# A recurrence's doubling step: half of one head's products move to the other partition half, in six groups a level

## What is computed

```
def step(state, inp):
    r_t, w_t, k_t, v_t, kk_t, a_t = inp
    sa = jnp.einsum('bhvk,bhk->bhv', state, -kk_t)
    state = (state * w_t[:, :, None, :]
             + sa[..., None] * (kk_t * a_t)[:, :, None, :]
             + v_t[..., None] * k_t[:, :, None, :])
    y = jnp.einsum('bhvk,bhk->bhv', state, r_t)
    return state, y
```

## Time and profile before

| | |
|---|---|
| median of three runs | 2886.83 us (2880.5 to 2887.5) |
| span of the profiled execution | 2890.0 us; no other time of it is given |
| TensorE, VectorE, ScalarE, GpSimd busy | 2784.7, 1962.0, 1370.0, 1435.9 us |
| granted clock of TensorE, mean | 0.985 of full speed |
| the recurrence in the span | about 1680 to 2120 us |

### The profile page before, as it was taken

The page is one execution under the profiler, slowest core; times in us unless marked ns, Lnnn a source line. Parts: engine busy times, 40 slices in busy tenths (PEclk is TensorE's granted clock), DMA queues, the critical chain, the costliest instruction groups (busy, mean ns, idle before and its releaser), DMA issues.

```text
span 2890.0 us, 63578 instructions
## 1 busy us (share of the span) xinstructions
PE 2784.7 (96%) x25936; PEld 2218.1 (77%) x25936; DVE 1962.0 (68%) x2814; ACT 1370.0 (47%) x2296; POOL 1435.9 (50%) x961
## 2 busy tenths in 40 slices
PE   8898899999999999998999999999999999999998
PEld 6544567887888888876678878988878788888887
DVE  6587888689777777788132347776647766656667
ACT  5476877235334433346433345666414443334445
POOL 0001000233777767774446636675552576677772
PEclk9899999999999999999999999999999999999999
DMA  8200000532332322331442411222312112111111
GB/s 300 77 1 16 1 2 2 212 106 62 88 102 73 93 81 83 93 113 32 160 146 88 161 60 55 76 85 64 112 36 59 44 48 69 44 44 58 57 45 73
DMA packets 194397, 225.29 MB, mean 78 GB/s; under 512 B 14862, under 2 KB 151649, under 8 KB 194209
## 3 DMA queue, kind: packets, MB, share of 16 engines
q1 hardware_dynamic: 182529, 180.66, 20.2%
q10 hardware_dynamic: 11680, 42.01, 4.0%
HBM read 185.15 MB, written 37.22 MB: 77 GB/s over the span
## 4 chain that ended last, share of the span: by engine, by line
PE 72%; DVE 9%; ACT 4%; issue 3%; POOL 2%; DMA 0%; ACTq 0%; DVEq 0%; SPq 0%; POOLq 0%
PE ps L148 18%; PE ps L149 18%; PE ps L150 18%; PE ps L3849 3%; DVE uc L1090 2%; PE ps L3858 2%; PE ps L2304 2%; PE ps L2293 1%; PE ps L2315 1%; PE ps L3778 1%; PE ps L3856 1%; ACT d_r L2446 1%; PE ps L3838 1%; DVE d_r L2706 1%; POOL w_lo L738 1%
## 5 line engine op out<-in xcount | busy, mean ns | idle before, releaser
L148 PE MATMUL ps<-x_hi,w_hi 128*128 128x512 f32 x1160 | 453.3, 391 | 2.9 <-POOL w_lo L738 2.8
L150 PE MATMUL ps<-x_hi,w_lo 128*128 128x512 f32 x1160 | 451.5, 389 | 0.0
L149 PE MATMUL ps<-x_lo,w_hi 128*128 128x512 f32 x1160 | 451.4, 389 | 0.0
L738 POOL TENSOR_TENSOR w_lo<-w_room,w_hi 128x512 fp32r<-128x512 f32 x188 | 287.7, 1543 | 232.4 <-ACT w_hi L1252 232.4
L738 POOL TENSOR_TENSOR w_lo<-sq_room,w_hi 128x512 fp32r<-128x512 f32 x182 | 285.8, 1581 | 218.9 <-ACT w_hi L1252 218.9
L1090 DVE SCALAR_TENSOR_TENSOR uc<-u,pc,uc 128x1024 f32<-128x1024 f32 x176 | 327.4, 1871 | 25.9 <-ACT uc L1266 15.6
L1078 DVE TENSOR_TENSOR u<-u,ps 128x512 f32<-128x512 f32 x228 | 151.1, 683 | 195.3 <-PE ps L150 170.9
L148 PEld LDWEIGHTS ps<-x_hi,w_hi 128*128 128x128 f32 x1160 | 217.7, 188 | 50.5 <-POOL w_lo L738 5.7
L148 PE MATMUL ps<-g_hi,w_hi 128*128 128x512 f32 x640 | 250.3, 391 | 6.5 <-DVE h L1156 6.2
L150 PEld LDWEIGHTS ps<-x_hi,w_lo 128*128 128x128 f32 x1160 | 217.7, 188 | 45.6
L149 PEld LDWEIGHTS ps<-x_lo,w_hi 128*128 128x128 f32 x1160 | 217.8, 188 | 44.8
(11 more groups left out here) (493 smaller groups left out, 6876.2 us busy)
## 6 DMA issues: line engine op xcount, KB each, us to landing
w_room<-in_f_w_up_dram SPq DMA_DIRECT2D x48, 512.0 KB, 5.0
rwkv_scratch<-rp_stage ACTq DMA_DIRECT2D x48, 512.0 KB, 3.5
sq_room<-in_f_w_up_dram SPq DMA_DIRECT2D x40, 512.0 KB, 4.6
ada_w<-in_ada_w_dram SPq DMA_DIRECT2D x80, 256.0 KB, 2.8
rc_raw<-rwkv_scratch SPq DMA_DIRECT2D x28, 512.0 KB, 3.9
d_ada_w<-in_ada_w_dram SPq DMA_DIRECT2D x24, 512.0 KB, 7.7
d_r<-in_ada_w_dram ACTq DMA_DIRECT2D x24, 512.0 KB, 6.4
sq_room<-in_f_w_down_dram SPq DMA_DIRECT2D x24, 512.0 KB, 4.4
```

Of the source, the lines that this page charges most:

```text
L148: pe.matmul(out, w_hi, x_hi, start=first, stop=False, skip_group_check=skip)
L149: pe.matmul(out, w_hi, x_lo, start=False, stop=False, skip_group_check=skip)
L150: return pe.matmul(out, w_lo, x_hi, start=False, stop=last, skip_group_check=skip)
L738: pool.tensor_tensor(slot_of(k.w_lo, s), src, slot_of(k.w_hi, s).bitcast(F32), ALU.subtract).then_inc(w_lo_done, 1)
```

## The change

- Half of the second head's products (blocks 4 to 7) use the other partition half: `far(h, x, c)` gives the side, and `removed_pe` writes the first l there.
- A level on TensorE is six groups of 16 products. The loop is rotated: the z of level 1 stand ahead of it (`first_z`), the body makes u and l of a level and z of the next, four times, and the u of level 5 stand behind it (`last_u`). The l products of level 5 are dropped.
- The first head's u, z and the second head's l are copied in two parts of 256 columns (PARTS = 2, 1), and their banks move; all of PSUM is one tensor so that one copy can read two banks. The key sums are four products of 256 columns in halves of banks 2, 3, 5 and 6, and the second pair of them also waits for the copy of y.
- ScalarE's order: log and root of the pair before move from level 3, behind both heads' copies, to level 5, between the u copies of the first and second head. turn moves from level 2 to level 5.
- VectorE's order: the key maxima move ahead of the levels, s1 behind level 1, s2 behind level 4, scans into levels 2 and 3.

```diff
+    def far(h, x, c):
+        return c if h and x >= QUARTER else 1 - c
...
+    def z_of(pe, h, x, c):
+        i = x // QUARTER
+        out = bank(4 + i if h else 4 + 2 * i)[:, part(x, 1 - h if i == 0 else 0)]
+        return pe.matmul(out[hs(far(h, x, c)), :], tg[hs(c), x, h, G_M, :], ul[hs(c), 0, h, x, :],
+                         start=True, stop=True)
+
+    def u_of(pe, h, x, c):
+        side, i = hs(far(h, x, c)), x // QUARTER
+        out = bank(2 * h + i)[:, part(x)]
+        return pe.matmul(out[hs(c), :], ul[side, 1, h, x, :], z[side, h, x, :],
+                         start=False, stop=False, skip_group_check=True)
+
+    def l_of(pe, h, x, c):
+        side = hs(far(h, x, c))
+        out = bank(x // QUARTER)[:, part(x, 1)] if h else bank(7)[:, at(x)]
+        return pe.matmul(out[side, :], z[side, h, x, :], ul[side, 1, h, x, :],
+                         start=False, stop=False, skip_group_check=True)
...
+    def first_z(pe, p):
+        for i in range(2):
+            if i and p + 1 < PAIRS:
+                pe.wait_ge(sem["max"], 2 * p + 4)
+            for x in quarter(i):
+                for c in range(2):
+                    a_last = z_of(pe, 0, x, 1 - c)
+                    if i:
+                        z_of(pe, 1, x, c)
+            a_last.then_inc(sem["z_ps"][0], 1)
+        pe.wait_ge(sem["z_sb"][0], 10 * p + 1)
+        for x in quarter(0):
             for c in range(2):
...
+                last = z_of(pe, 1, x, c)
+        last.then_inc(sem["z_ps"][1], 1)
...
     def level_pe(pe, p, lv):
...
+        pe.wait_ge(sem["l_sb"][0], lv + 4 * p)
+        for i in range(2):
+            pe.wait_ge(sem["z_sb"][0], lv * 2 + (10 * p + i - 1))
+            pe.wait_ge(sem["l_sb"][1], lv * 2 + (8 * p + i - 1))
             begun(pe)
...
+            ul_a(pe, i)
+        pe.wait_ge(sem["z_sb"][1], lv + 5 * p)
+        begun(pe)
+        u_b(pe)
+        for i in range(2):
+            pe.wait_ge(sem["u_sb"][0], lv * 2 + (10 * p + i - 1))
             begun(pe)
...
+            z_a_l_b(pe, i)
+        pe.wait_ge(sem["u_sb"][1], lv + 5 * p)
+        pe.wait_ge(sem["z_sb"][0], lv * 2 + (10 * p + 1))
+        begun(pe)
+        z_b(pe)
+
+    def last_u(pe, p):
+        pe.wait_ge(sem["l_sb"][0], 4 * p + 5)
+        for i in range(2):
+            pe.wait_ge(sem["z_sb"][0], 10 * p + 9 + i)
+            pe.wait_ge(sem["l_sb"][1], 8 * p + 9 + i)
+            ul_a(pe, i, False)
+        pe.wait_ge(sem["z_sb"][1], 5 * p + 5)
+        u_b(pe)
...
             banks_opened(pe, p)
-            with pe.Fori(1, 6) as lv:
+            first_z(pe, p)
+            with pe.Fori(1, LV[-1]) as lv:
                 level_pe(pe, p, lv)
+            last_u(pe, p)
...
             for lv in LV:
...
+                u_act(act, p, lv, 0)
+                if p and lv == LV[-1]:
+                    log_act(act, p - 1)
+                    root_act(act, p - 1)
+                u_act(act, p, lv, 1)
+                if lv < LV[-1]:
+                    la_act(act, p, lv)
+                    lb_act(act, p, lv)
+                if more and lv in (1, 2):
+                    ln_act(act, q, lv - 1)
+                if more and lv in (3, 4):
+                    rs_act(act, q, lv - 3)
+                if lv == LV[-1]:
+                    turn_act(act, p, 0)
+                    turn_act(act, p, 1)
             tail_act(act, p)
...
+            if more:
                 for i in range(2):
...
+                    max_dve(dve, q, i)
             for lv in LV:
...
+                for h in range(2):
+                    levels_dve(dve, p, lv, h)
+                if p and lv == 1:
+                    for i in range(2):
+                        s1_dve(dve, p - 1, i)
+                if p + 2 < PAIRS and lv in (2, 3):
+                    scan_dve(dve, p + 2, lv - 2)
+                if p and lv == 4:
+                    for i in range(2):
+                        s2_dve(dve, p - 1, i)
```

More of the change, by code:

```diff
@@ L101, in alloc @@
     k.nm_small = [k.sb(f"nm_small{i}", [P, 3, TT]) for i in range(3)]
[L103 removed]
+    k.ps_all = stack.enter_context(nc.psum_tensor("ps", [P, 4, S], F32))
+    k.ps = [k.ps_all[:, i, :] for i in range(4)]
     k.w_room = k.sb("w_room", [P, 2, S])
@@ L3586, in rkw_act, with sums_of @@
         act.activation(rkw, heads2[:, :], ACT.Copy, scale=col("b_r_k", q)).then_inc(sem["bon"], 1)
+    def sums_of(q, i):
+        if q == 0:
+            return bank(6 + i).rearrange("p (b c) -> p b c", b=2)
+        return bank_pair((2, 5)[i], slice(HALF // 2, HALF))
     def max_dve(dve, q, i):
         dve.wait_ge(sem["sum"], 2 * q + i + 1)
-        dve.tensor_scalar(kk[:, halves(i)], bank(6 + i), 1e-24, None, ALU.max).then_inc(sem["max"], 1)
+        dve.tensor_scalar(kk[:, halves(i)].rearrange("p (b c) -> p b c", b=2), sums_of(q, i), 1e-24, None, ALU.max
+                          ).then_inc(sem["max"], 1)
     def kk_dve(dve, q, i):
@@ L3608, in sums_pe @@
         for i in range(2):
-            pe.matmul(bank(6 + i), same[:, :], kk[:, halves(i)], start=True, stop=True).then_inc(sem["sum"], 1)
+            if q >= 2 and i:
+                pe.wait_ge(sem["y_sb"], q - 1)
+            for n in range(2):
+                cols = slice((2 * i + n) * 2 * P, (2 * i + n + 1) * 2 * P)
+                last = pe.matmul(sums_of(q, i)[:, n, :], same[:, :], kk[:, cols], start=True, stop=True)
+            last.then_inc(sem["sum"], 1)
     def bon_one(pe, q, x):
@@ new lines, in part @@
+    def part(x, right=0):
+        return at(x % QUARTER + QUARTER * right)
+    def z_of(pe, h, x, c):
[8 more added lines that the diff above has]
+                         start=False, stop=False, skip_group_check=True)
@@ new lines, in ul_a, with u_b @@
+    def ul_a(pe, i, l_too=True):
+        for x in quarter(i):
+            for c in range(2):
+                u_last = u_of(pe, 0, x, c)
+                if l_too:
+                    l_last = l_of(pe, 0, x, 1 - c)
+        u_last.then_inc(sem["u_ps"][0], 1)
+        if l_too and i:
+            l_last.then_inc(sem["l_ps"][0], 1)
+    def u_b(pe):
+        for x in quarter(0):
+            for c in range(2):
+                u_of(pe, 1, x, c)
+                last = u_of(pe, 1, QUARTER + x, c)
+        last.then_inc(sem["u_ps"][1], 1)
@@ new lines, in z_a_l_b, with z_b, opened @@
+    def z_a_l_b(pe, i):
+        for x in quarter(i):
+            for c in range(2):
+                z_last = z_of(pe, 0, x, 1 - c)
+                l_last = l_of(pe, 1, x, c if i else 1 - c)
+        z_last.then_inc(sem["z_ps"][0], 1)
+        l_last.then_inc(sem["l_ps"][1], 1)
+    def z_b(pe):
+        for x in quarter(0):
+            for c in range(2):
+                z_of(pe, 1, x, 1 - c)
+                last = z_of(pe, 1, QUARTER + x, c)
+        last.then_inc(sem["z_ps"][1], 1)
+    def opened(pe, out, c, side_of):
+        pe.matmul(out[hs(c), at(0)], id64[hs(side_of), :], same[hs(side_of), hs(1 - side_of)],
+                  start=True, stop=False, skip_group_check=True)
@@ L3863, in banks_opened, with last_opened @@
+    def last_opened(pe, p):
+        pe.wait_ge(sem["g2_sb"], 2 * BLK * (p + 1))
+        if p:
+            pe.wait_ge(sem["s_sb"], UPD * p)
+        for c in range(2):
+            for i in range(2):
+                opened(pe, bank(2 + i), c, (c, 1 - c)[i])
+            opened(pe, bank(7), c, 1 - c)
     def banks_opened(pe, p):
-        pe.wait_ge(sem["g2_sb"], 2 * BLK * (p + 1))
         pe.wait_ge(sem["g3_sb"], BLK * (p + 1))
@@ L3867, in banks_opened @@
             pe.wait_ge(sem["y_sb"], p)
[L3868 to L3872, removed]
+        for c in range(2):
+            for i in range(2):
+                opened(pe, bank(i), c, c)
     def begun(pe):
```

114 lines of the change are left out of this document (48 added, 66 removed).

## The result

The changed kernel takes 2929.2 us (median of four runs, 2924.8 to 2936.0) where the kernel before takes 2884.8 (four runs, 2880.5 to 2887.5): a ratio of 1.0152, 95% interval 1.0132 to 1.0171. It is 44 us slower. The prediction said 2926, range 2898 to 2945. The profiled execution took 2926.9 us, with a span of 2925.2.

What follows compares the result with a forecast made beforehand. TensorE, 72% of the chain, was taken as the bound. Pairs 1 to 6 +25.8, pair 7 +3.2, pair 0 -2.1, clock +14, absorbed pauses -1.5: +39 on 2886.83, giving 2926 us, range 2898 to 2945.

Steps and rivals of the forecast that it cites:

- The doubling, 2.3 us saved: TensorE's five levels in a pair: second head's last u ends 19.33 us after the first z, against 21.66.
- The slack of 0.19 us: ScalarE in the levels: part of a u copy's 1.02 us delay behind load and Ln that costs nothing, leaving 0.83 lost.
- the pause that the chain calls "issue": TensorE's pause at 1908.26, counted in level 1 of a doubling: left in unchanged at 0.60 us.
- Log and root, net 4.3 us later: Pairs 1 to 6, log and root in level 5 with two loads: transposes start at 29.8 us after first z, not 25.53.
- TensorE idle 1.9 us, then 4.7: Tail: TensorE waits 1.9 us for the second head's u copy, then 4.7 for GpSimd's passes before the transposes.
- The clock, +2.0 a pair: Tail after the 4.7 us idle: TensorE at half clock for 5.4 us, costing 2.0 us a pair, bounds 0 and 2.7.
- Pair 7, +3.2 us: Last pair, without Ln, Exp, pause and bonus: transposes at 27.4 us after the first z, against 24.2.
- Pauses absorbed, -1.5: Code pauses that fall in a tail may be absorbed by the idle time: 1.5 us less, an estimate.
- Pair 0, -2.1: First pair, with no norm to wait for: doubling of 19.2 us against 21.28, 2.1 us saved.
- 1, the norm not late: Rival at the tail's transposes: norm ready in time, every pair keeps its 2.3 us, 2869 us; chance 0.08.
- 2, no loads: Rival on ScalarE: no table loads in log and root or at Ln and Exp, 2884 us; chance 0.04.
- 3, groups not four abreast: Rival in TensorE's levels: 0.94 us a group, level 6.0 us, 80 us more, about 3005; chance 0.02.

Runs made afterwards that it cites:

- experiments 1, 2 and 4: Log and root back in level 3 of changed kernel, 2885.8 us; moved to level 5 in kernel before, 2942.5; as plain copies, 2913.4; behind both u copies, 2929.1.
- experiment 3: Changed kernel with products that nobody reads filling TensorE's idle time in pairs 1 to 7: 2915.9 us, ratio 1.0099 to the kernel before.
- e1_log_at_3: Changed kernel with log and root, and VectorE's sums of squares, back in level 3: 2885.8 us, ratio 0.9998 to the kernel before.
- e3, experiment 2: Changed kernel with log and root of all pairs but the last as plain copies needing no table: 2913.4 us, ratio 1.0087 to the kernel before.
- e5_log3_unrolled: e1_log_at_3 with TensorE's loop over the levels written out as four bodies: 2950.9 us, ratio 1.0209 to the kernel before.

## Why the prediction was right

**The doubling, 2.3 us saved.** Half right. In the changed kernel the last product of the levels starts 19.1 us after the first z in pair 0, 20.6, 20.4, 22.7, 19.9, 19.9, 19.5 in pairs 1 to 6, and started at 21.2 to 21.9 before. Where nothing disturbs, a pass takes 3.66 us; I had 3.46. The hold ahead of the last group is 0.36 (I took 0.30), the loop's turn with its waits 0.45 (0.35), the six groups 2.85 (2.81). The passes behind the loads for Ln and Exp took 4.28 and 3.97 us in pair 0 (4.28 and 4.08 expected), with holds for ScalarE's u copy; in pair 4 the first of the two holds is for VectorE's z copy behind its scan, which I did not have. (The slack of 0.19 us in that term should be 0.15, 0.94 less 0.79.) The term that was mis-sized is "the pause that the chain calls 'issue'": I left in 0.6 us a doubling as a constant, and in the denser code it is 1.5 and 0.6 us in pair 1 and 2.0 in pair 3. With it the last product of pair 3 starts 0.8 us later than before instead of 2.3 earlier. Over the eight doublings 8.7 us were saved; the prediction's terms (2.3 in six pairs, 2.1 in pair 0 and 4.4 in pair 7) make 20.

**Log and root, net 4.3 us later.** Right, and the cause is shown by experiments 1, 2 and 4. The transposes of pairs 1 to 6 start 5.2, 4.7, 7.0, 4.4, 4.3 and 4.2 us later, 29.8 together where I had 25.8; the excess lies in pairs 1 to 3, whose pauses are the longest. Pair 4: root's end at 23.1 (said 22.5), GpSimd's passes to 29.9 (29.7), transposes 30.0 (29.8), next pair's keys to 37.0 (36.9). Both loads are there as the rows said, and removing them brought 16 to 18 us. The Trainium skill ("ScalarE: Activation LUTs", section "Table sets: the hidden batching unit") lists a set with both functions, by which they would not be there. The traces differ: between 1690 and 2130 us ScalarE loads a table 18 times before and 28 times in the changed kernel, once at each turn between Ln and Exp.

**TensorE idle 1.9 us, then 4.7.** The first is 1.94 from start to start in pairs 1 to 6, of which 1.7 idle. The second, measured so, is 4.6 in pairs 2 and 5, 3.9 in pair 7 and 3.0 to 3.1 in the others: there the clock had already fallen behind the first idle, and the tail products, at half clock, filled part of the second. I had put the low clock behind the second idle alone.

**The clock, +2.0 a pair.** The size is right by experiment 3 (13 to 16 us in 7 pairs), though stretches of half clock are 3.4 to 13.7 us long, not 5.4, and much of them lies in waits.

**Pair 7, +3.2 us.** Too small. The transposes are at 31.8 after the first z against 24.2 before, +7.6: the last product of the levels started at 21.7 instead of 17, with pauses of 0.8 and 1.4 us and 3.4 us of half clock behind them. I had taken pair 7 as free of pauses because the kernel before shows none in its loop's first pass there.

**Pauses absorbed, -1.5.** Those in the tails are absorbed, more than I had: the idle times over 0.4 us called issue behind the doublings fell from 4.7 to 0.7 us. But those in the doublings grew from 3.1 to 10.0 us. They lie ahead of root and push the whole chain, so that the pauses together cost time.

**Pair 0, -2.1.** The doubling is 2.15 us shorter; from first z to first z it was -3.0.

Together: the recurrence up to pair 7's first z is 36.3 us longer; my terms for it (25.8 - 2.1 + 12 - 1.5) make 34.2. Behind it 8.5 against 5.2. So 3 of the 5 us that are missing are pair 7's. That the sum comes so near is in part luck: the doublings saved less than half of what I had, and the tails' absorbed pauses made up for some of it.

**Rivals.** 1, the norm not late: its condition was made true by e1_log_at_3, and its 2869 did not come: with the norm on time the time is 2886. So the 2.3 us a pair, on which it rested, were not there to be had; the doublings gave 0.9, and pair 7 took most of that again. 2, no loads: e3 took away log's and root's and left those at Ln and Exp, and gave 2913 instead of 2884; the place costs 26 without them. No run leaves out all four. 3, groups not four abreast: 0.47 us for 32 records in all profiles speaks against it.

## What to carry to other kernels

A faster inner stage pays only if the work that other engines do beside it keeps its place: here a log and a root moved two levels down cost 43 us, more than twice the 18 us that the stage was to give. Follow the engine that waits for the moved result to its end, and count the table loads that the new order makes. Before making straight code denser, see what its waits called issue are: here the written-out passes brought seven packets of code a doubling, the loop two or three.

## What the runs showed that was not expected

- Straight code of 64x64 products four abreast came at one block of 252 instructions (16384 bytes) in about 4.1 us (e5_log3_unrolled), while TensorE ran it in 1.98. Writing out four or five passes in eight places costs 65 us in the changed order and 72 in the kernel before.
- ScalarE's tables: a change between Ln and Exp was a load of 1.283 us wherever the order made one; with plain copies in their place (experiment 2) there was none.
- In the changed kernel half clock came already with the first idle, of 1.7 us, in pairs 1, 3, 4 and 6 (pair 4: products at 0.50 from 1936.78 on), and only behind the second in pairs 2 and 5. In the kernel before, a stretch of 3.0 us with next to no products had kept 1.00. Filling the idle time with products that nobody reads kept 1.00 in the tails of pairs 1 to 6 (experiment 3).
- The eight doublings vary by 1 to 2 us each between kernels with the same code on TensorE, by where its pauses fall. Runs of one kernel spread over 10 to 20 us of 2886, so that a difference of 0.1% is not told from none even with 12 runs.
